# One change to the start and to the two norms of a fused transformer block: order of the first loads, granularity of the first matmuls, and where squares are summed

## The reference

```python
h   = rms_norm(x, norm1_g);  z = h @ w_in          # pool | q | k | v | forget columns
q, k = rms_norm(q), rms_norm(k)                    # per head of 64
x   = x + concat[pool_mixer(z_pool), forgetting_attention(q, k, v, log_f)] @ w_out
h   = rms_norm(x, norm2_g)
x   = x + peer_ffn(h)     # 8 heads, product keys, top 16 of 16384 experts, gelu(u.h) weighted v
```

## Time and profile before

| | before |
|---|---|
| median of 3 runs | 1501.5 us (1501.4 to 1502.32) |
| profiled execution, its time | 1501.01 us |
| profiled execution, span first to last instruction | 1499.0 us |
| TensorE busy | 1482.6 us, 99% |
| VectorE / ScalarE / GpSimd busy | 75% / 39% / 65% |
| mean DMA rate | 255 GB/s |

### The profile page before, as it was taken

The page is one execution under the profiler, slowest core; times in us unless marked ns, Lnnn a source line. Parts: engine busy times, 40 slices in busy tenths (PEclk is TensorE's granted clock), DMA queues, the critical chain, the costliest instruction groups (busy, mean ns, idle before and its releaser), DMA issues.

```text
span 1499.0 us, 20613 instructions
## 1 busy us (share of the span) xinstructions
PE 1482.6 (99%) x7613; PEld 1301.6 (87%) x7613; DVE 1122.2 (75%) x1917; ACT 580.2 (39%) x792; POOL 971.5 (65%) x525
## 2 busy tenths in 40 slices
PE   8999999999999999999999999999999999999998
PEld 5766678889999999999999999988888888888887
DVE  3467634176999999869999999388777777777774
ACT  5565335233333333434444444333333333333332
POOL 4231134344688778876666665578878888887883
PEclk9999999999999999999999999999999999999999
DMA  5221023223587878898999997799888888888883
GB/s 201 94 71 64 29 98 120 80 75 120 168 266 265 279 262 261 305 332 271 356 364 351 353 355 248 273 385 351 344 344 317 341 345 340 319 344 347 316 302 123
DMA packets 122006, 381.53 MB, mean 255 GB/s; under 512 B 11864, under 2 KB 28376, under 8 KB 121952
## 3 DMA queue, kind: packets, MB, share of 16 engines
q1 hardware_dynamic: 70096, 202.64, 38.2%
q0 software_dynamic: 36864, 134.23, 24.6%
q10 hardware_dynamic: 14992, 44.06, 7.4%
HBM read 336.84 MB, written 44.06 MB: 254 GB/s over the span
## 4 chain that ended last, share of the span: by engine, by line
PE 97%; DVE 1%; issue 1%; ACT 1%; DMA 0%; SPq 0%; DVEq 0%
PE bank L643 28%; PE bank L644 28%; PE bank L645 28%; PE bank L853 6%; PE bank L738 1%; PE bank L659 1%; PE bank L785 1%; PE bank L758 1%; PE wide L748 1%; PE wide L643 0%; PE wide L645 0%; PE wide L644 0%; PE bank L866 0%; DMA vec<-vecs_dram 0%; DVE pad L1042 0%
## 5 line engine op out<-in xcount | busy, mean ns | idle before, releaser
L409 POOL TENSOR_TENSOR wl<-raw,wh 128x1024 fp32r<-128x1024 f32 x211 | 514.6, 2440 | 401.2 <-ACT wh L436 400.0
L643 PE MATMUL bank<-hh,wh 128*128 128x384 f32 (+1 forms) x1184 | 422.2, 357 | 0.0
L644 PE MATMUL bank<-hl,wh 128*128 128x384 f32 (+1 forms) x1184 | 409.9, 346 | 0.0
L645 PE MATMUL bank<-hh,wl 128*128 128x384 f32 (+1 forms) x1184 | 409.4, 346 | 0.0
L644 PE MATMUL bank<-wl,Wh 128*128 128x512 f32 x768 | 300.7, 392 | 0.0
L643 PE MATMUL bank<-wh,Wh 128*128 128x512 f32 x768 | 300.0, 391 | 0.0
L645 PE MATMUL bank<-wh,Wl 128*128 128x512 f32 x768 | 298.4, 389 | 0.0
L436 ACT ACTIVATE wh<-raw 128x1024 fp32r<-128x1024 f32 x225 | 237.0, 1054 | 154.0 <-PE bank L645 137.4
L644 PEld LDWEIGHTS bank<-hl,wh 128*128 128x128 f32 x1184 | 222.7, 188 | 9.4 <-issue 1.7
L643 PEld LDWEIGHTS bank<-hh,wh 128*128 128x128 f32 x1184 | 222.6, 188 | 9.3 <-issue 1.7
L645 PEld LDWEIGHTS bank<-hh,wl 128*128 128x128 f32 x1184 | 222.1, 188 | 8.7
(11 more groups left out here) (169 smaller groups left out, 1673.8 us busy)
## 6 DMA issues: line engine op xcount, KB each, us to landing
raw<-uT_dram SPq DMA_DIRECT2D x128, 512.0 KB, 4.4
xraw<-v_dram SPq DMA_DIRECT2D x72, 512.0 KB, 9.2
raw<-v_dram SPq DMA_DIRECT2D x56, 512.0 KB, 9.2
a_dram<-act_a ACTq DMA_DIRECT2D x64, 384.0 KB, 5.7
wf<-a_dram SPq DMA_DIRECT2D x32, 768.0 KB, 6.9
raw<-wst_dram SPq DMA_DIRECT2D x41, 512.0 KB, 3.2
gates_dram<-gbuf ACTq DMA_DIRECT2D x32, 512.0 KB, 7.0
gt<-gates_dram SPq DMA_DIRECT2D x32, 512.0 KB, 4.1
```

The lines of the kernel that those rows point to most:

```text
L409: pool.tensor_tensor(wl[:, n % SPLIT, :], raw_of(n), wh[:, n % SPLIT, :].bitcast(F32), ALU.subtract).then_inc(w_lo, 1)
L643: pe.matmul(dst, ah, bh, start=start, stop=False)
L644: pe.matmul(dst, ah, bl, start=False, stop=False)
L645: return pe.matmul(dst, al, bh, start=False, stop=stop)
```

## The change

At the start SyncE issues chunk 0, then `vec`, two quarters of x, chunk 1, the other two quarters, and `cst` last, with a semaphore of its own for `vec`. ScalarE rounds chunk 0 before it looks at x, and chunk 3 before the root rather than behind it. The value chunks take tile by tile (loop over kk outside), each tile when its `ml` is there; chunks 0 and 1 run before TensorE looks at the squares. TensorE multiplies a zeroed buffer five times at the start (five float32 matmuls). Both norms' squares are added tile to tile on VectorE (`add_square`, between `zc` and `ml`), and one matmul with ones (`sum_all`) adds over the partitions: for the first norm behind value chunk 1, for the second inside the first early chunk ahead of its k = 5. The sums for q and k stay as they were.

```diff
+ZEROS = 5
...
-            load_x(0)
-            sp.dma_start(cst[:, :], consts).then_inc(in_consts, 16)
-            sp.dma_start(vec[:, :], vecs).then_inc(in_consts, 16)
             for n in range(END_W):
...
                 sp.dma_start(raw_of(n), weights(n)).then_inc(landed(n)[0], 16)
                 if n == 0:
-                    for i in range(1, 4):
-                        load_x(i)
+                    sp.dma_start(vec[:, :], vecs).then_inc(in_vecs, 16)
+                    load_x(0)
+                    load_x(1)
+                elif n == 1:
+                    load_x(2)
+                    load_x(3)
+                    sp.dma_start(cst[:, :], consts).then_inc(in_consts, 16)
...
                 if what == "norm1":
+                    hi_to(0)
                     for k in range(KD):
...
+                if what == "norm1":
+                    hi_to(SPLIT - 1)
                 if what in ("norm1", "ss", "norm2"):
                     act.wait_ge(var_ready, roots + 1)
...
-            pe.wait_ge(in_consts, 32)
+            def sum_all(used):
+
+                pe.wait_ge(sq_used, used)
+                pe.matmul(bank[SS][:, :], ones, newt[:, :], start=True, stop=True).then_inc(ss_done, 1)
+
+            pe.wait_ge(zeroed, 1)
+            for _ in range(ZEROS):
+                pe.matmul(bank[PV][:, :], pm[:, 0:P], pm[:, :], start=True, stop=True)
...
                 if what == "norm1":
-                    for k in range(KD):
-                        sum_square(k, ones, k == 0, k == KD - 1)
-                        if k == 3:
-                            run("proj", VALUES[0], [])
+                    for n in VALUES[:2]:
+                        run("proj", n, [])
+                    pe.wait_ge(in_consts, 16)
+                    sum_all(KD)
...
-                        pe.wait_ge(g_lo, 2 * pair + 2)
-                        for b in range(TB):
-                            for kk in range(2):
-                                k = 2 * pair + kk
+                        for kk in range(2):
+                            k = 2 * pair + kk
+                            pe.wait_ge(g_lo, k + 1)
+                            for b in range(TB):
...
-                    if n > OUT_W:
-                        sum_square(SQ_OUT + n - OUT_W - 1, ones, n == OUT_W + 1, False)
...
-                elif what == "norm2":
-                    sum_square(SQ_OUT + KD - 1, ones, False, True)
                 elif what == "early":
+                    def first_early(k):
+                        if k == KD - 3:
+                            sum_all(3 * KD)
+                        pe.wait_ge(g_lo, KD + k + 1)
...
+            dve.memset(pm[:, :], 0.0).then_inc(zeroed, 1)
...
-            dve.wait_ge(in_consts, 32)
+            dve.wait_ge(in_vecs, 16)
...
+            def add_square(k, i):
+
+                if k:
+                    dve.wait_ge(sq_ready, i + 1)
+                if k == 1:
+                    dve.tensor_tensor(bank[SS][:, :], sq[:, (i - 1) % 4, :], sq[:, i % 4, :], ALU.add).then_inc(sq_used, 2)
+                elif k:
+                    dve.wait_ge(sq_used, i)
+                    dve.tensor_tensor(newt[:, :] if k == KD - 1 else bank[SS][:, :], bank[SS][:, :], sq[:, i % 4, :],
+                                      ALU.add).then_inc(sq_used, 1)
...
                 dve.tensor_scalar(zc[:, k % 2, :], x[:, k, :], vec[:, g + k:g + k + 1], None, ALU.mult)\
                    .then_inc(g_ready, 1)
+                add_square(k, k if i < KD else SQ_OUT + k)
                 lo_part(i, k, g_hi, g_lo, high, low, zc[:, k % 2, :])
```

More of the change, by code:

```diff
@@ L199, in program @@
         mask = cst[:, C_MASK:C_MASK + P]
-        in_consts, in_pool, in_keys = sem("in_consts"), sem("in_pool"), sem("in_keys")
+        in_consts, in_vecs, in_pool, in_keys = sem("in_consts"), sem("in_vecs"), sem("in_pool"), sem("in_keys")
         in_x = [sem(f"in_x{i}") for i in range(4)]
@@ L205, in program @@
         w_hi, w_lo, w_used = sem("w_hi"), sem("w_lo"), sem("w_used")
-        sq_ready, sq_used = sem("sq_ready"), sem("sq_used")
+        sq_ready, sq_used, ss_done = sem("sq_ready"), sem("sq_used"), sem("ss_done")
         var_ready, ln_ready, root_ready = sem("var_ready"), sem("ln_ready"), sem("root_ready")
@@ L220, in program @@
         pool_prod, pool_hi, pool_lo, x1_ready = sem("pool_prod"), sem("pool_hi"), sem("pool_lo"), sem("x1_ready")
-        out_done = sem("out_done")
+        out_done, zeroed = sem("out_done"), sem("zeroed")
         sc_prod, sc_saved, identr_ready = sem("sc_prod"), sem("sc_saved"), sem("identr_ready")
@@ L465, in _ @@
                         act.wait_ge(f_ln, 1)
-                        act.wait_ge(in_consts, 32)
+                        act.wait_ge(in_consts, 16)
                         act.preload_act_table_set("natural_log")
@@ L497, in _ @@
                     act.wait_ge(pool_prod, i + 1)
-                    act.wait_ge(in_consts, 32)
+                    act.wait_ge(in_vecs, 16)
                     act.activation(hh[:, i, :], bank[SS][:, :], ACT.Copy, scale=vec[:, PS + i:PS + i + 1])\
@@ L767, in run @@
                         project(bank[S_BANK + j][:, 0:DT], (EARLY_W + j) % SPLIT, mh, ml,
-                                (lambda k: pe.wait_ge(g_lo, KD + k + 1)) if j == 0 else None, at=slice(FIRST, T))
+                                first_early if j == 0 else None, at=slice(FIRST, T))
             for stage in stages:
-                if stage[:2] != ("proj", VALUES[0]):
+                if stage[:2] not in [("proj", n) for n in VALUES[:2]]:
                     run(*stage)
@@ L948, in _ @@
                 if what in ("norm1", "ss", "norm2"):
-                    dve.wait_ge(sq_used, {"norm1": KD, "ss": SQ_QK + i + 1, "norm2": 3 * KD}[what])
+                    dve.wait_ge(*{"norm1": (ss_done, 1), "ss": (sq_used, SQ_QK + i + 1), "norm2": (ss_done, 2)}[what])
                     fence()
```

## The result

| | before | changed |
|---|---|---|
| median (6 runs each) | 1501.39 us | 1494.06 us (1493.83 to 1494.81) |
| ratio | | 0.995, 95% interval 0.994 to 0.996 |
| span of the profiled execution | 1499.0 us | 1492.0 us |
| start of "columns" (L679, now L692) | 39.05 us | 39.06 us |
| first query chunk | 248.06 us | 241.23 us |

The changed kernel is 7.3 us faster by the medians. The forecast was 1492.9, in a range from 1491.0 to 1496.3. The two last lines of the table split the gain of the traces, whose spans differ by 7.0 us: none of it had been made when the value chunks ended; 6.8 us of it were made by the first query chunk.

The account below looks back on a forecast made before the run. TensorE's own work was taken as the bound (97% of the chain). Gains of 6.87 (second norm) + 1.7 (start) = 8.6 us took the 1501.01 us execution to 1492.4, plus 0.5 for the median: 1492.9, range 1491.0 to 1496.3.

Parts of the forecast that it names:

- its first half: First norm and value chunks at the start: L679 starts at 36.75 to 37.95 against 39.05, gain taken as 1.7 us.
- its second half: Second norm, output projection to first query chunk: sums leaving TensorE gain 5.16 + 1.71 = 6.87 us.
- the rival with the fallen clock: Value chunk 1: pace halves behind the new 4.3 us gap, 1.8 us net lost, 1494.7 us; chance 0.25.
- Second norm, 6.87 us: Output projection and passage to the early stage: removed sums gain 5.16 + 1.71 = 6.87 us.
- Six sums gone from between the chunks: Output projection chunks 1 to 6: each loses one `sum_square` of 0.86 us, 5.16 us in all.
- The passage to the early stage and on to the first query chunk: Behind output chunk 7: 2.57 us goes, one sum of 0.86 us stays inside the early stage; gain 1.71 us.
- 0.8 us were to be left at the first query chunk: First query chunk: its `wl` ends at 245.6, TensorE wants it at 246.35, so the later root chain costs nothing.
- Additions at no cost: VectorE, between `zc` and `ml`: each 0.70 us addition of squares fits the 0.70 us wait for `mh`.
- First norm, 1.7 us: Start to L679: changed loads, roundings and value chunks gain 1.1 to 2.3 us, taken as 1.7.
- W: Start, GpSimd: end of the first `wl`, chunk 0's landing + 3.5, so 7.45 to 8.65 us.
- the quarter lands a little behind 6: Start, loads: first quarter of x, third in the queue with 1038.5 KB including what is ahead, lands a little behind 6 us.
- the meeting of `zc` with GpSimd: Start, VectorE: the first `zc` meets GpSimd's first `wl` and ends about 0.34 us behind it.
- The zeros, "cost nothing": Start, TensorE: zeros run before the first `wl` ends and cost nothing; full pace for chunk 0 only lengthens idle time.

Follow-up runs that it names:

- experiment 8: Changed kernel with the second norm's `sum_all` moved to the head of the second early chunk; 1494.81 us, ratio 0.9953.
- Experiment 1: Kernel before with only the second norm's half of the change (`add_square` for its tiles, one sum), start as before; 1494.93 us, ratio 0.9953.
- experiment 9: Kernel with chunks rounded behind tiles 2, 4, 6 and sum behind value chunk 2, now first quarter of x issued ahead of `vec`; 1489.64 us, ratio 0.9914.
- 2, first half: Kernel before with only the start's part of the change, `sum_square` behind each output chunk as before; 1501.48 us, ratio 0.9999.
- 3, gap filled: Changed kernel with four more float32 matmuls of zeros between value chunks 0 and 1; 1492.68 us, ratio 0.9941.
- experiment 4: Changed kernel with `ZEROS = 0`, no matmuls of zeros at the start; 1494.22 us, ratio 0.9949.
- experiment 7: Changed kernel with the value chunks waiting for both tiles again, loop order as changed; 1493.06 us, ratio 0.994.
- 5: Changed kernel with ScalarE rounding value chunks 1 to 3 behind tiles 2, 4, 6; 1494.61 us, ratio 0.9952.
- 6: Changed kernel with chunks 1 to 3 rounded behind tiles 2, 4, 6, `sum_all` behind value chunk 2, chunks 4 and 5 rounded before the root; 1489.17 us, ratio 0.9915.
- experiment 11: Kernel with chunks rounded behind tiles 2, 4, 6 and sum behind value chunk 2, now with `ZEROS = 0`; 1490.39 us, ratio 0.9935.
- 10: Kernel with chunks rounded behind tiles 2, 4, 6 and sum behind value chunk 2, now first quarter of x issued before chunk 0; 1492.55 us, ratio 0.9937.

## Why the forecast held, and where its parts did not

The forecast's total was 1.2 us too low, its first half was wrong and its second half right. The measured 1494.06 lies nearer to the rival with the fallen clock (1494.7) than to the forecast: it was in the range in part because the range had been made to hold that rival. The range's upper end, 1496.3, is also 1.0 us above what its terms give (1494.7 + 0.6).

*Second norm, 6.87 us: right.* Six sums gone from between the chunks: forecast 5.16, measured 229.03 - 223.89 = 5.14 with the start unmoved. The passage to the early stage and on to the first query chunk: forecast 1.71, measured (248.06 - 229.03) - (241.23 - 223.89) = 1.69. `sum_all` waited for nothing; the root chain came 0.9 us later, forecast 1.0; 0.8 us were to be left at the first query chunk, and experiment 8 used them up and paid the rest. Experiment 1 has the 7.0 us by itself, in its median.

*Additions at no cost: right.* The tile pitch stayed at 1.79 us in the first norm. In the second each waited 0.18 us for its square, beside idle time.

*First norm, 1.7 us: wrong, measured 0.0.* W came out at 7.72, inside the interval, and by it L692 should have been at 37.0; it was at 39.06. Two terms failed.

The first is the landing of x: "the quarter lands a little behind 6" was worked out from bytes in the queue alone. It landed at 8.3. From 4.0 to 4.5 us the queues moved 82 GB/s, and in the two half microseconds from 5 to 6 107 and 147. With x ahead of `vec` it lands at 6.63 (experiment 9). So the place behind `vec`, 14.5 KB in 128 short rows, cost about 1.3 us between these two traces, and 0.3 to 1.7 us over all nine that have it; why it does is not settled. This also undid the next step, the meeting of `zc` with GpSimd, which did not take place; with the two errors against each other chunk 1 started at 20.13 in place of W + 11.5 = 19.2. It costs 0.9 us.

The second is the clock: the rival named first, "the clock falls in the new gap", is what happened. It was priced at 1.8 us net from the length of the slow stretch at the very start. Chunk 1 took 27.30 - 20.13 = 7.17 us in place of 5.45, and 0.4 of the 1.7 lay in front of chunk 2's `wl`: 1.2 to 1.3 net. The slow stretch was 3.3 us and not 4.06. With the landing of x subtracted, six traces that round and run the value chunks in the changed kernel's order put the price at 1.1 us:

| trace | first square of x | L692 | difference | clock in chunk 1 |
|---|---|---|---|---|
| changed | 8.32 | 39.06 | 30.74 | fell |
| 2, first half | 8.78 | 39.55 | 30.77 | fell |
| 8, late sum | 8.22 | 38.98 | 30.76 | fell |
| 3, gap filled | 8.23 | 37.88 | 29.65 | held |
| 4, no zeros | 7.65 | 37.32 | 29.67 | held |
| 7, both tiles | 7.36 | 37.01 | 29.65 | held |

By the rule of the Trainium skill, "TensorE: Matmul & The Clock Gate", section "Why this matters for your kernels", that a long enough gap between bursts of matmuls puts the clock back to half, this rival was to be the forecast. The traces agree: behind the gap of 4.0 us it fell (changed, 2, 8), with the gap filled it did not (3). I gave it 0.25 on the ground that TensorE had been busy for most of the 15 us before, which did not protect it.

Without the late x and the clock, 39.06 - 0.9 - 1.1 = 37.06, and the steps gave 37.0. So the chain by which chunks 1 to 3 wait for ScalarE's roundings was read rightly. I had taken it as given, though, and priced the change within it; experiments 5 and 6 show it to be what held the start, together with the place of the sum: moving three roundings alone brought nothing once the landing of x is subtracted (5: 30.71), because the gap went to `sum_all`; moving them, the two next and the one sum brought 5.1 us (6: 39.06 to 33.99), where the change itself had brought nothing.

*The zeros, "cost nothing": wrong.* The prediction had it that full pace in chunk 0 would only lengthen the idle time behind it, and so it was; but the longer gap is what made the clock fall. Without the zeros L692 came 1.1 us earlier, the landing of x set aside (experiment 4). With the gap closed they are worth 1.1 us (experiment 11). No total shows either clearly.

## What to carry to other kernels

Work taken from an engine that does not wait in that stretch came back in full (6.8 of 6.9 us here), if one checks what is due next and how much it has to spare. Work moved forward in a stretch that waits for something else only makes a longer wait, and on TensorE a wait can cost twice, since the clock may fall behind it: so find first what ends the last wait (here the order of another engine's roundings), move that, and only then fill what is left.

## What the runs showed of the hardware that was not expected

At the start the clock fell when work had resumed and not in the gap: 0.3 us (8), 0.6 (2), 0.8 (10), 1.2 (changed) and 1.4 us (5) into the next burst, each time for about 3.4 us. Behind gaps of 3.1 (10), 3.2 (5) and 4.0 us (changed, 2, 8) it fell in every trace, behind gaps of 1.9 to 2.4 us (2, 4, 6, 7) at the start in none. But in the attention it fell in four of thirteen traces at the end of, or just behind, three waits that come to 1.2 us with one small matmul between one and the next, while the other nine traces have the same waits and kept it. So the length of the gap alone does not decide. Each of these four falls took back about 1.6 us, more than one at the start cost.

The same transfer at the same place in the order landed at different times: the first quarter of x, behind chunk 0 and the 14.5 KB of `vec` in short rows, between 7.36 and 8.78 us over nine traces, and at 6.63 ahead of `vec` (experiment 9, one trace). In the changed kernel's trace the half microseconds from 3.5 to 6 us moved 82 to 156 GB/s, where the kernel before had 263 to 376; in experiment 7's they moved 156 to 344.
